# Gate projections placed between attention steps, with the head-pair loop written out and one buffer for cached keys and values

## The reference, cut to what matters

```python
h = jnp.einsum('bsd,de->bse', x, w_in)
qa, ka, va, qb, kb, vb, ga, gb = jnp.split(h, _col_splits(), axis=-1)
...
return qa, ka, va, qb, kb, vb, jax.nn.sigmoid(ga), jax.nn.sigmoid(gb)
...
br_a = jnp.einsum('bse,ed->bsd', o_a.reshape(N, S, A_Q_W), w_branch_a)
br_b = jnp.einsum('bse,ed->bsd', o_b, w_branch_b)
mix = jnp.einsum('bsd,de->bse', ga * br_a + gb * br_b, w_out)
h = layer_norm(ALPHA * x + mix, ln1_g, ln1_b)
u = jnp.square(jax.nn.relu(jnp.einsum('bsd,df->bsf', h, w_ff1) + b_ff1))
f = jnp.einsum('bsf,fd->bsd', u, w_ff2) + b_ff2
```

## Time and profile before

| | us |
|---|---|
| median of three runs | 1941.76 |
| lowest and highest of them | 1939.97, 1941.88 |
| span of the profiled execution | 1940.0 |
| TensorE busy in it | 1854.4 (96%) |
| DVE busy | 922.6 (48%) |
| ACT busy | 743.5 (38%) |
| POOL busy | 100.1 (5%) |

### The profile page before, as it was taken

One profiled execution on the slowest core, in us unless ns is written; L12 is line 12 of the kernel. 1 busy time (PEld: TensorE's weight loads), 2 busy tenths in 40 slices (PEclk: granted clock), 3 DMA queues, 4 the chain that ended last, 5 costly groups with the idle time before them and its releaser, 6 DMA issues.

```text
span 1940.0 us, 34466 instructions
## 1 busy us (share of the span) xinstructions
PE 1854.4 (96%) x12750; PEld 1781.7 (92%) x12750; DVE 922.6 (48%) x1217; ACT 743.5 (38%) x1038; POOL 100.1 (5%) x208
## 2 busy tenths in 40 slices
PE   7999999999988998999969999999999999999993
PEld 7999999999985656999959999999999999999992
DVE  5455443433345665664484444444344444444444
ACT  5454543333333444333343433333333433334322
POOL 0000000100002221100000000000000000000000
PEclk9999999999998888999969999999999999999996
DMA  8555555765665554655517666665766666666631
GB/s 251 153 151 145 175 168 162 242 180 171 178 199 214 209 215 177 200 188 178 167 52 245 204 215 219 217 219 202 238 198 219 203 215 207 229 207 213 216 108 54
DMA packets 270891, 368.76 MB, mean 190 GB/s; under 512 B 11920, under 2 KB 264528, under 8 KB 267904
## 3 DMA queue, kind: packets, MB, share of 16 engines
q1 hardware_dynamic: 250368, 249.17, 42.3%
q0 software_dynamic: 9088, 106.90, 14.3%
q10 hardware_dynamic: 11392, 12.13, 1.9%
HBM read 356.02 MB, written 70.71 MB: 220 GB/s over the span
## 4 chain that ended last, share of the span: by engine, by line
PE 94%; DVE 3%; issue 1%; ACT 1%; DMA 0%; POOL 0%; DVEq 0%; ACTq 0%; SPq 0%; POOLq 0%
PE psM L945 28%; PE psM L946 28%; PE psM L947 28%; PE psM L993 1%; PE psM L1006 1%; PE psO L1051 1%; PE psO L1038 1%; PE psT L1019 1%; DVE s_r L870 1%; PE psO L1048 1%; DVE s_r L879 1%; PE psM L1002 0%; PE psT L965 0%; PE psO L1053 0%; PE psO L1066 0%
## 5 line engine op out<-in xcount | busy, mean ns | idle before, releaser
L647 DVE TENSOR_TENSOR s_wlo<-s_raw,s_whi 128x1024 fp32r<-128x1024 f32 x468 | 573.4, 1226 | 833.1 <-ACT s_whi L422 825.5
L422 ACT ACTIVATE s_whi<-s_raw 128x1024 fp32r<-128x1024 f32 x468 | 495.4, 1059 | 955.0 <-PE psM L947 930.6
L945 PE MATMUL psM<-s_xhi,s_whi 128*128 128x320 f32 x1248 | 387.8, 311 | 9.9 <-DVE s_xlo L652 9.9
L947 PE MATMUL psM<-s_xhi,s_wlo 128*128 128x320 f32 x1248 | 386.4, 310 | 0.0
L946 PE MATMUL psM<-s_xlo,s_whi 128*128 128x320 f32 x1248 | 386.4, 310 | 0.0
L945 PE MATMUL psM<-s_hhi,s_whi 128*128 128x320 f32 x1024 | 317.8, 310 | 9.2 <-DVE s_hlo L865 8.6
L946 PE MATMUL psM<-s_hlo,s_whi 128*128 128x320 f32 x1024 | 317.4, 310 | 0.0
L947 PE MATMUL psM<-s_hhi,s_wlo 128*128 128x320 f32 x1024 | 317.4, 310 | 0.0
L945 PE MATMUL psM<-s_uhi,s_whi 128*128 128x320 f32 x1024 | 316.4, 309 | 0.0
L946 PE MATMUL psM<-s_ulo,s_whi 128*128 128x320 f32 x1024 | 316.4, 309 | 0.0
L947 PE MATMUL psM<-s_uhi,s_wlo 128*128 128x320 f32 x1024 | 316.4, 309 | 0.0
(11 more groups left out here) (164 smaller groups left out, 1613.6 us busy)
## 6 DMA issues: line engine op xcount, KB each, us to landing
s_raw<-in_w_ff_dram SPq DMA_DIRECT2D x256, 512.0 KB, 3.8
s_raw<-in_w_in_dram SPq DMA_DIRECT2D x156, 512.0 KB, 3.8
s_kcache<-in_kT_b_dram POOLq DMA_DIRECT2D x8, 2448.0 KB, 8.4
s_vcache<-in_v_b_dram POOLq DMA_DIRECT2D x8, 2304.0 KB, 8.1
s_raw<-in_w_out_dram SPq DMA_DIRECT2D x32, 512.0 KB, 3.5
out_b_s_dram<-in_cache_b_kv_dram POOLq DMA_DIRECT2D x16, 1008.0 KB, 6.2
s_raw<-in_w_branch_a_dram SPq DMA_DIRECT2D x16, 512.0 KB, 3.5
gates_scratch<-s_gstage ACTq DMA_DIRECT2D x16, 320.0 KB, 2.5
```

The costliest lines, as they stand in the source:

```text
L422: act.activation(whi[:, slot], raw[:, slot], ACT.Copy).then_inc(hi_done, 1)
L647: dve.tensor_tensor(wlo[:, slot], raw[:, slot], whi[:, slot].bitcast(F32), ALU.subtract).then_inc(lo_done, 1)
L945: pe.matmul(out, wh, hi[:, t0 + k], start=first and k == 0, stop=False)
L947: mm = pe.matmul(out, wl, hi[:, t0 + k], start=False, stop=last and k == KT - 1)
```

## The change

The sixteen gate groups no longer run ahead of attention. Groups 0 and 1 and half of group 2 run first; then each step of attention is followed by one gate chunk, through group 14; group 15 follows the last unit. `gates_and_attention` writes out that order for all 48 steps, so that the loop over head pairs is gone. Gate groups 2 to 14 accumulate in `psM[1]`, and all scores go to `psM[0]` alone, so that the scores of unit U now wait until unit U-1 is masked. On DVE `back` comes before `front`. ACT takes the sigmoid of a gate group inside a step of attention, every fourth step. Each engine's weight split for a chunk three ahead stands behind its part of the step. The copies to `QB`, `KB`, `VB` and `QA` are gone, since TensorE reads the pair's queries, keys and values where they are. Cached keys and values take turns in one buffer, `kvbuf`, that no longer lies over the input tokens; values are loaded when SB's scores are done, the next keys when SB's sums are done. The attention output `oT` now lies over the queries.

```diff
-            [("kcache", [P, 4, CK, KN], F32), ("vcache", [P, CK, 512], F32),
-             ("vnewb", [NG * DT, 512], F32), ("kca", [P, KN], F32)],
...
+             ("kvbuf", [P, 4 * CK * KN], F32), ("vnewb", [NG * DT, 512], F32), ("kca", [P, KN], F32)],
...
+        def gate_bank(n):
+
+            return psM[0 if n in (1, NGATE - 1) else 1]
...
+        def gates_and_attention(gate, between, attend, end):
+
+            for n in range(2):
+                for k in range(4):
+                    gate(n, k)
+                between(n)
+            for n in range(2, NGATE - 1):
+                for k in range(4):
+                    if n > 2 or k >= 2:
+                        attend(at(4 * (n - 3) + k))
+                    gate(n, k)
+            end()
+            for k in range(4):
+                gate(NGATE - 1, k)
...
+            pool.wait_ge(kcopy, 7)
             load_k(0)
             add_new_keys(0)
-            load_v(0)
...
+            load_va(0)
+            for n in range(DB):
+                pool.wait_ge(scores, 6 * n + 5)
+                load_v(n)
+                if n < DB - 1:
+                    pool.wait_ge(sums, n + 1)
+                    pool.wait_ge(scores, 6 * n + 6)
+                    load_k(n + 1)
...
+            def sigmoids(n):
+
+                act.wait_ge(chunk_done, 4 * (G_G + n) + 4)
+                if n >= 2:
+                    act.wait_ge(gate_stored[n % 2], 16 * (n // 2))
+                act.activation(gstage[:, n % 2], gate_bank(n)[:, :, 0:NTOK], ACT.Sigmoid).then_inc(gate_evac, 1)
...
             def attend(at):
+                s = at(0)
                 if at(1):
                     exps(*at(1))
+                if s and s[2] % 4 == 0:
+                    sigmoids(s[2] // 4 + 2)
...
+                if s:
+                    turned_probs(*s)
...
-                    dve.tensor_copy(QB[:], q4[:, :, bass.ds(j, 1), 0:256].rearrange("p g a n -> p g (a n)"))
-                    dve.tensor_copy(KB[:], k4[:, :, bass.ds(j, 1), 0:256].rearrange("p g a n -> p g (a n)"))
...
             def attend(at):
+                if at(0):
+                    back(*at(0))
                 if at(1):
                     front(*at(1))
-                back(*at(0))
...
-                wait(pe, masked, U - 1)
+                wait(pe, masked, U)
...
+                elif k == 0:
+                    pe.wait_ge(gate_evac, n)
+                chunk(4 * (G_G + n) + k, k, gate_bank(n), xhi, xlo, 4 * k, k == 0, k == 3)
```

More of the change, by code:

```diff
@@ L45 @@
 KN = P + DT
+NGATE = 16
 def program(nc, a, o):
@@ L211, in program, with at, one @@
         NSINK = len(SINKED)
[L212 to L231, removed]
+        LAST = 4 * NU
+        def at(s):
+            def one(d):
+                U = s + d
+                return (U // NU, U % NU, U) if 0 <= U < LAST else None
+            return one
+        def gates_and_attention(gate, between, attend, end):
[11 more added lines that the diff above has]
+                gate(NGATE - 1, k)
         def wait(eng, s, value):
@@ L371, in _ @@
             pool.wait_ge(pv, 4 * NU)
[L372 to L378, removed]
+            for q in range(2):
+                pool.wait_ge(gate_stored[q % 2], 16 * (4 + q // 2 + 1))
+                load_gates(q, q % 2)
+            for q in range(2, 8):
+                pool.wait_ge(m_sum, q - 1)
+                pool.wait_ge(gate_stored[q % 2], 16 * (4 + q // 2 + 1))
+                load_gates(q, q % 2)
             def load_x(q, e):
@@ L538, in o_evac @@
                     tile = j + (8 if kind == "B" else 4 * e)
-                    last = act.activation(oT[part, bass.ds(tile, 1), P * qb:P * qb + P],
-                                          ps[part, 0:P].rearrange("p (a n) -> p a n", a=1), ACT.Copy)
+                    last = act.activation(oT[part, tile, P * qb:P * qb + P], ps[part, 0:P], ACT.Copy)
                 elif kind == "SB":
@@ L562, in attend, with end @@
                     (sums_evac if UNITS[at(-1)[1]][0] == "SB" else o_evac)(*at(-1))
-                turned_probs(*at(0))
-            units(act, attend)
-            o_evac(3, NU - 2, 4 * NU - 2)
-            o_evac(3, NU - 1, 4 * NU - 1)
-            act.wait_ge(o_out, 4 * NU)
-            for j in range(3):
-                act.activation(ohi[:, 4 * j:4 * j + 4], oT[:, 4 * j:4 * j + 4], ACT.Copy).then_inc(o_hi, 1)
+                if s:
+                    turned_probs(*s)
+            def end():
+                split(G_BR - 1, 3)
+                sigmoids(NGATE - 2)
+                o_evac(3, NU - 2, LAST - 2)
+                o_evac(3, NU - 1, LAST - 1)
+                act.wait_ge(o_out, LAST)
+                for j in range(3):
+                    act.activation(ohi[:, 4 * j:4 * j + 4], oT[:, 4 * j:4 * j + 4], ACT.Copy).then_inc(o_hi, 1)
+            gates_and_attention(gate, between, attend, end)
+            sigmoids(NGATE - 1)
             with act.Fori(0, 2) as i:
@@ L696, in stage_first @@
                 dve.wait_ge(zeroed, 2)
-                for k in range(4):
-                    stage(0, k, k)
             def step(g, i, c, kind, turn):
@@ L791, in back, with gate, between, end @@
                 last.then_inc(normed, 1)
-            front(0, 0, 0)
-            dve.wait_ge(gate_stored[0], 16 * 8)
-            dve.wait_ge(gate_stored[1], 16 * 8)
+            def gate(n, k):
+                if n < 2 or n == NGATE - 1:
+                    split(G_G + n + 1, k)
+                elif k > 0:
+                    split(G_G + n + 1, k - 1)
+                elif n > 2:
+                    split(G_G + n, 3)
+            def between(n):
+                if n == 1:
+                    stage_first()
             def attend(at):
+                if at(0):
+                    back(*at(0))
                 if at(1):
                     front(*at(1))
-                back(*at(0))
-                if at(4) and at(4)[1] != 0:
+                if at(0) and at(4) and UNITS[at(4)[1]][0] in ("SB", "SA"):
                     stage(*at(4))
-                if at(3) and at(3)[1] == 0:
-                    stage(*at(3))
-            units(dve, attend)
-            for j in range(3):
-                dve.wait_ge(o_hi, j + 1)
-                dve.tensor_tensor(olo[:, 4 * j:4 * j + 4], oT[:, 4 * j:4 * j + 4], ohi[:, 4 * j:4 * j + 4].bitcast(F32),
-                                  ALU.subtract).then_inc(o_lo, 1)
+            def end():
+                split(G_BR - 1, 3)
+                for j in range(3):
+                    dve.wait_ge(o_hi, j + 1)
+                    dve.tensor_tensor(olo[:, 4 * j:4 * j + 4], oT[:, 4 * j:4 * j + 4], ohi[:, 4 * j:4 * j + 4].bitcast(F32),
+                                      ALU.subtract).then_inc(o_lo, 1)
+            gates_and_attention(gate, between, attend, end)
             with dve.Fori(0, 2) as i:
@@ L1068, in turn_sums, with gate, between @@
                 mm.then_inc(pv, 1)
[L1070 to L1073 removed]
+            def gate(n, k):
+                if k == 0 and n == 0:
+                    pe.wait_ge(evac[1], E_BR // 2)
+                elif k == 0 and n == 1:
+                    pe.wait_ge(evac[0], E_BR // 2 + 1)
+                elif k == 0 and n == 2:
+                    pe.wait_ge(gate_evac, 1)
+                elif k == 0 and n == NGATE - 1:
+                    pe.wait_ge(masked, LAST)
+                elif k == 0:
+                    pe.wait_ge(gate_evac, n)
+                chunk(4 * (G_G + n) + k, k, gate_bank(n), xhi, xlo, 4 * k, k == 0, k == 3)
+            def between(n):
+                if n == 0:
+                    turn(G_G - 1, 0, G_G - 1)
             def attend(at):
                 if at(2):
+                    if at(2)[2] == 0:
+                        pe.wait_ge(gate_evac, 2)
                     unit_scores(*at(2))
@@ L1081, in attend, with end @@
                     unit_values(*at(-1))
-                turn_probs(*at(0))
-            units(pe, attend)
-            turn_sums(3, NU - 2, 4 * NU - 2)
-            unit_values(3, NU - 1, 4 * NU - 1)
+                if at(0):
+                    if at(0)[2] == 0:
+                        pe.wait_ge(turned_out, 13)
+                    turn_probs(*at(0))
+            def end():
+                turn_sums(3, NU - 2, LAST - 2)
+                unit_values(3, NU - 1, LAST - 1)
+            gates_and_attention(gate, between, attend, end)
             with pe.Fori(0, 2) as i:
```

226 lines of the change are left out of this document (105 added, 121 removed).

## The result

The changed kernel takes 1947.64 us in the median (1946.61 to 1948.81, 7 runs), against 1941.88 for the kernel before (1939.51 to 1946.26, 7 runs): a ratio of 1.0034, 95% interval 1.0024 to 1.0044. The profiled execution has a span of 1946.3 us (before: 1940.0).

A forecast was written before the change was run, and what follows sets the result against it. TensorE was taken as busy throughout the gates, with attention losing time to waits and 1.2 GHz. Branch products 13 us later (781 against 768.5) plus 13 for clock made +26 on 1940.0: 1966, median 1967; range 1950 to 1985.

The forecast's parts named there:

- rival 2: In the 48 steps, ACT's lateness and the slow clock cost next to nothing: 1931 us; chance 0.17 with what lies between.
- The chain: Per step, ACT's copy, both weight splits, normalising and mask take 4.2 us against a 3.52 us chunk: TensorE stands 0.7.
- Rival 1: In the 48 steps the chain hides under the chunk and TensorE sets the pace: 319 us, total 1897; chance 0.08.
- TensorE's own work: In the 48 steps, attention at 18.8 us per six units, 150 in all, plus a 3.52 us chunk per step.
- the scores ahead and the values behind: Around the 48 steps: about 2.5 us of scores before the first, about 2 of last sums and values after.
- ACT inside the step: Sigmoids leave 2.3 of 2.47 us in eight B0 and SB steps, 18, plus 6 other lateness: 24, bounds 0 to 30.
- the further 6 us of lateness in B0: In B0 steps, ACT late for reasons other than the sigmoid: an estimated 0.7 us in each of eight.
- The clock: Work of the rebuilt stretch at 1.2 GHz: 13 us, a quarter of the 53 at attention's present share.
- Rival 3: In the rebuilt stretch the clock stays as attention had it: 53 us in place of 13, total 2007; chance 0.15.
- Costed at nothing: In the steps, key and value loads priced at zero; if one step late, up to 7 us in each of 8 passes.
- the second table load: On ACT, the load back to the exponential, behind the weight split: zero, or 15 us for 12 without that cover.
- rival 4: On ACT, each of 12 table switches also pays a 1.38 us drain: 17 more, total 1984; chance 0.05.

The follow-up runs named there:

- mask-first kernel: Changed kernel with DVE doing the mask of unit s+2, then the normalising of s+1, ahead of its weight split: 1890.0 us, ratio 0.9741 to the kernel before.
- the two kernels above: Changed kernel with gates apart from attention: shared key/value buffer, 2004.24 us; values in their own buffer and all sixteen groups first, 1936.13 us.
- the run with the longer chain: Changed kernel with one more 128x768 copy on DVE ahead of the mask in each of the 48 steps: 1971.14 us.

## Why the prediction was right in sign and wrong in size

The prediction followed the right chain and found the right sign, but its time is 19 us too long; the measured one lies between rival 2 (1931) and the forecast, where 0.17 was given. The branch products start at 777.1, where the prediction had 781 + 13 for the clock = 794. Its terms against what the runs show:

- *The chain*: right. 0.7 us a step were 33 in 48; the gaps are 35.9, of which 2.7 stay in the kernel without the chain, so 33.2. The links and their order are those of the rows above. Only the mean of 0.7 was forecast, and the steps differ: 41 scores wait, not 48, from 0.2 us (B0 behind SA) to 1.1 (SB), not longest in every fourth step, and behind the five chunks at 1.2 GHz the wait is 0.25 at most. Rival 1 was not what happened, but it is what the kernel does when the chain is cut: its step pace, 319 us for 48, against 314.75 measured, and 1897 against 1890.
- *TensorE's own work*: 150 + 169 = 319, against 314 in the mask-first kernel, so 5 too much. I had priced 48 full steps and then added the scores ahead and the values behind, 2.5 and 2, a second time; but attention's matmuls came out 12 us shorter than 150 in all and the chunks 4 longer than 169, and that further difference I can't explain.
- *ACT inside the step*: this is the step that failed, mis-sized: 24, measured 11.4. I let 2.3 of a sigmoid's 2.47 us stand in each B0 and SB step, as a delay of the copy in the chain. What waits is the next gate chunk, for its bank. By the time TensorE comes to it, values and transpositions have covered part of the sigmoid: in the step shown ACT is done with the exponentials at 420.65 and TensorE with the transposition at 421.42, 0.8 later; and the issue of the transfer, which was in the 2.47, stands behind the release of the bank. So 1.30 stands in each SB step and 1.1 to 2.0 in the four of B0. That A0 hides all of it was right. For the further 6 us of lateness in B0 I find no wait.
- *The clock*: 13, measured 182.4 - 173.0 = 9.4, in five chunks of 5.1 us and more. Rival 3 (0.86 as before) did not come: without chunks between its steps, attention has 0.77 and 0.91 in the two kernels above, with them 0.97. That the clock's losses come with the waits, and not with attention's thin work as such, the mask-first run shows: the same instructions, nearly without waits, at 1.00.
- Attention's own matmuls take 141.8 us, against 138.4 in the mask-first kernel: 3.4 that no term held. They come with the waits; how is not shown.

Together -5 - 12.6 - 3.6 + 3.4 + 0.6 for the chain is -17 in the 48 steps, which is the miss at the branch products. Another 2 us are given back behind them. In the kernel before, the first branch products followed a wait of 3.90 us, and the timeline has them 0.26 us apart at first (granted clock 0.50 from 768.5 to 771):

```profile
768.52 0.63 PE L945 MATMUL psM<-s_ohi,s_whi 128*128 128x320 f32 x1 [3.90 <-DVE s_olo L810]
768.95 0.47 PE L946 MATMUL psM<-s_olo,s_whi 128*128 128x320 f32 x1
769.21 0.47 PE L947 MATMUL psM<-s_ohi,s_wlo 128*128 128x320 f32 x1
```

Now they follow group 15 without a wait, 0.14 apart (clock 1.00):

```profile
777.08 0.31 PE L964 MATMUL psM<-s_ohi,s_whi 128*128 128x320 f32 x1
777.22 0.31 PE L965 MATMUL psM<-s_olo,s_whi 128*128 128x320 f32 x1
```

So a start that is 8.6 later leads to a normalisation that is 7.3 later (its first sum at 978.36, before at 971.08). I had left this out. The remaining 1 us lies in the stages behind and is not explained.

*Costed at nothing*: the second table load cost nothing that shows, 24 more loads are there in the steps (the whole span has 14 ahead of sigmoids and 13 ahead of exponentials, where there was one of each), and rival 4's drain is not: the table load starts 0.03 us behind the instruction ahead of it (420.68 after 420.47 + 0.18), and the sigmoid 0.01 us behind the load (421.97 after 420.68 + 1.28). Rival 4 also counted 12 switches where its steps have 24. The loads of keys and values are hidden, as forecast, but only by the chunks: 50 us of waits stand where these are taken away. There the price I gave, up to 7 us in each of 8 passes, was of the right size.

Against the kernel before, the change had 51 us to give (1941 - 1890) and gave -6. Alternation removes the thin stretches, the waits for the loads and the wait for the output's split, and one order of three calls on one engine gave all of it back.

## What to carry to other kernels

When two streams of work are woven together, write down for each engine's queue what the first blocked instruction holds up. A closed chain through several engines' queues can set the pace even where each is busy for less than half of the time (here DVE for 165 and ACT for 170 of 372 us). Put work that is needed soonest (the mask that frees a bank) ahead of work that has slack (a split needed three chunks later); here a reordered DVE won 58 us and a reordered ACT 52 on the changed kernel. A buffer may be shared if something long stands between its two uses; measure it with that cover taken away before the cover is moved.

## What the runs showed of the hardware

In these runs a table load does not wait for the input of the function behind it. In the mask-first kernel it ran from 411.37 to 412.65 while the sigmoid's chunk was still being computed, and the sigmoid then waited 0.19 us for that chunk. There the load hides behind the wait for the chunk; in the changed kernel, where ACT comes late, it does not.

Waits of a microsecond or two can cost TensorE more than their own length. In the changed kernel all five chunks at 1.2 GHz are in B0 steps: four behind a wait of 1.1 to 2.0 us for the sigmoid, the fifth (at 533.73) with no wait just ahead of it, only 0.72 ahead of the scores of its step. A step with waits of 0.70 ahead of the scores and 1.56 ahead of the chunk goes on with a chunk at 1.2 GHz that is 1.5 us longer, and steps with 0.20 and 1.30 do not. In the run with the longer chain all eight B0 steps have such a chunk, and of the four SB steps with waits of some 0.67 and 1.31 two have chunks of 5.03 and 5.16 us and two of 3.62. In the mask-first kernel, where one wait of 0.7 is left, no chunk is at 1.2 GHz. What decides between such steps is open.
